# A two-layer hybrid decoder trunk: SiLU's table, the copies out of PSUM, the weight rounding and the small loads in another order

## What is computed

```python
for layer in range(DEPTH):
    h = rms_norm(x, norm_w[layer])
    proj = jnp.einsum('bsd,de->bse', h, w_in[layer])          # 4096 x 11792
    (g_q, g_k, g_v, g_a, s_q, s_k, s_v, d_q, d_k, d_v, r_x, gate) = split_cols(proj, IN_SPLITS)
    y = jnp.concatenate([gla_mixer(g_q, g_k, g_v, g_a, ...), swa_mixer(s_q, s_k, s_v, ...),
                         diff_mixer(d_q, d_k, d_v, ...), rglru_mixer(r_x, ...)], axis=-1)
    y = y * jax.nn.silu(gate)
    x = x + jnp.einsum('bse,ed->bsd', y, w_out[layer])        # 4096 x 4096
```

## Time and profile before

| | |
|---|---|
| median of 3 runs | 2942.19 us (2942.0 to 2942.79) |
| the profiled execution | 2942.81 us, span 2941.1 us |
| granted TensorE clock | 1.0 |
| TensorE matmul busy | 2913.7 us (99%) |
| VectorE busy | 1585.7 us (54%) |
| ScalarE busy | 1465.4 us (50%) |
| DMA | 546 MB, 186 GB/s over the span |

### The profile page before, as it was taken

The page is one execution under the profiler, slowest core; times in us unless marked ns, Lnnn a source line. Parts: engine busy times, 40 slices in busy tenths (PEclk is TensorE's granted clock), DMA queues, the critical chain, the costliest instruction groups (busy, mean ns, idle before and its releaser), DMA issues.

```text
span 2941.1 us, 34608 instructions
## 1 busy us (share of the span) xinstructions
PE 2913.7 (99%) x13381; PEld 2404.3 (82%) x13381; DVE 1585.7 (54%) x2098; ACT 1465.4 (50%) x2077; POOL 59.3 (2%) x106
## 2 busy tenths in 40 slices
PE   8999999999999999999999999999999999999999
PEld 6888888888888888888878888888888888888887
DVE  6545455555666446444554455555556664554444
ACT  5344455545556555444554444455555665553333
POOL 2000000000000000000000000000000000000000
PEclk9999999999999999999999999999999999999999
DMA  7665556666555665766666655566655555666665
GB/s 232 179 191 165 160 171 179 188 189 182 169 164 164 187 184 186 225 218 198 222 178 193 187 159 164 174 188 182 183 178 176 158 172 179 192 201 208 222 222 164
DMA packets 282964, 546.47 MB, mean 186 GB/s; under 512 B 17752, under 2 KB 22496, under 8 KB 282800
## 3 DMA queue, kind: packets, MB, share of 16 engines
q1 hardware_dynamic: 272560, 524.88, 58.1%
q0 software_dynamic: 5552, 17.26, 1.9%
q10 hardware_dynamic: 4688, 2.13, 0.3%
HBM read 535.81 MB, written 8.39 MB: 185 GB/s over the span
## 4 chain that ended last, share of the span: by engine, by line
PE 97%; ACT 1%; DMA 0%; DVE 0%; issue 0%; SPq 0%; ACTq 0%
PE main L1128 91%; PE mixer L1128 5%; ACT L382 1%; PE mixer L1343 0%; DMA w_raw<-in_w_in 0%; ACT stage L382 0%; DVE w_lo L697 0%; PE mixer L1168 0%; ACT w_hi L375 0%; PE mixer L1279 0%; PE mixer L1319 0%; PE mixer L1199 0%; PE mixer L1307 0%; PE mixer L1306 0%; PE mixer L1269 0%
## 5 line engine op out<-in xcount | busy, mean ns | idle before, releaser
L1128 PE MATMUL main<-w_hi,act 128*128 128x512 f32 x7936 | 2523.4, 394 | 17.1 <-ACT stage L382 13.6
L697 DVE TENSOR_TENSOR w_lo<-w_raw,w_hi 128x1024 fp32r<-128x1024 f32 x992 | 1204.8, 1224 | 1088.4 <-ACT w_hi L375 1081.5
L1128 PEld LDWEIGHTS main<-w_hi,act 128*128 128x128 f32 x7936 | 1491.0, 188 | 333.4 <-issue 19.9
L375 ACT ACTIVATE w_hi<-w_raw 128x1024 fp32r<-128x1024 f32 x992 | 1041.0, 1058 | 1070.2 <-PE main L1128 1039.5
L1128 PE MATMUL main<-w_lo,act 128*128 128x512 f32 x3968 | 1545.8, 390 | 0.0
L1128 PEld LDWEIGHTS main<-w_lo,act 128*128 128x128 f32 x3968 | 746.3, 188 | 149.2
L677 DVE SCALAR_TENSOR_TENSOR act<-act_T,par,act 128x256 fp32r<-128x256 f32 x96 | 42.0, 478 | 13.2 <-ACT act L357 13.1
L929 DVE TENSOR_TENSOR mix<-mix,main 128x512 f32<-128x512 f32 x32 | 22.0, 687 | 42.7 <-PE main L1128 42.7
L791 DVE TENSOR_SCALAR mix<-mix_Y,small 128x128 f32<-128x128 f32 x32 | 7.7, 282 | 67.7 <-ACT small L389 67.7
L357 ACT ACTIVATE act<-act_T,par 128x256 fp32r<-128x256 f32 x96 | 42.9, 495 | 0.1
L1128 PE MATMUL mixer<-act_T,mix 128*128 128x128 f32 (+1 forms) x256 | 39.6, 288 | 0.0
(11 more groups left out here) (238 smaller groups left out, 1092.4 us busy)
## 6 DMA issues: line engine op xcount, KB each, us to landing
w_raw<-in_w_in SPq DMA_DIRECT2D x736, 512.0 KB, 3.7
w_raw<-in_w_out SPq DMA_DIRECT2D x256, 512.0 KB, 3.7
out<-mix POOLq DMA_DIRECT2D x15, 512.0 KB, 3.2
mix<-in_x POOLq DMA_DIRECT2D x8, 512.0 KB, 6.0
mix<-out POOLq DMA_DIRECT2D x8, 512.0 KB, 5.9
mix_Y<-in_x SPq DMA_DIRECT2D x7, 512.0 KB, 9.2
act_T<-in_lru_w_r ACTq DMA_DIRECT2D x16, 64.0 KB, 2.6
act_T<-in_lru_w_i ACTq DMA_DIRECT2D x16, 64.0 KB, 2.7
```

Source lines behind the costliest of these rows:

```text
L375: act.activation(w_hi[:, n % HI, :, :], w_raw[:, n % RAW, :, :], ACT.Copy).then_inc(w_hi_ready, 1)
L697: dve.tensor_tensor(w_lo[:, n % LO, :, :], w_raw[:, n % RAW, :, :], w_hi[:, n % HI, :, :].bitcast(F32), ALU.subtract).then_inc(w_lo_ready, 1)
L1128: return pe.matmul(out_, lhsT, rhs, start=start, stop=stop, skip_group_check=True)
```

## The change

Five moves; no instruction of the computation is added or left out.

1. `preload_act_table_set("silu_and_others")` stands ahead of the waits of copy 0 of a gate chunk.
2. `project` and `evacuate` take the token half t: copy 0 is made at g = 0, copy 1 at g = 1. ScalarE's order becomes `hi(j,0)`, copy 0, what is hooked in at g = 0, `hi(j,1)`, copy 1, what is hooked in at g = 1.
3. In chunk 0 of layer 0 `hi` and `lo` run one group ahead: group 0's before the first split of x, group g + 1's at g, ahead of the split of x for g + 1.
4. The 23 row DMAs, and with them the first `load_rank`, wait for `w_used` 6 (six groups of chunk 0 done).
5. The rank product moves from the end of chunk 0 to the end of chunk 2 (`J_RANK` 2), its rounding to chunk 1 (g = 12 and 14) and the copy of its result to chunk 3.

Cut to its core:

```diff
+    J_RANK = J_GV
@@ gpsimd
-            def rows(dst, src):
-                pool.dma_start(dst, src).then_inc(rows_in, 16)
...
+            pool.wait_ge(w_used, 6)
+            def rows(dst, src):
+                pool.dma_start(dst, src).then_inc(rows_in, 16)
...
             load_rank(0)
@@ scalar
-            def evacuate(layer, j, dst, func):
+            def evacuate(layer, j, t, dst, func):
                 n = layer * CHUNKS + j
-                act.wait_ge(main0_ready, n + 1)
-                act.activation(dst[:, 0, :], main[0][:, :], func, scale=rstd[:, 0:1]).then_inc(main_free, 1)
-                act.wait_ge(w_used, n * NG + NG)
-                act.activation(dst[:, 1, :], main[1][:, :], func, scale=rstd[:, 1:2]).then_inc(main_free, 1)
+                if t == 0:
+                    act.wait_ge(main0_ready, n + 1)
+                else:
+                    act.wait_ge(w_used, n * NG + NG)
+                act.activation(dst[:, t, :], main[t][:, :], func, scale=rstd[:, t:t + 1]).then_inc(main_free, 1)
...
-            def project(layer, j, g):
-                if g != 1 or not 1 <= j <= J_OUT:
-                    return
+            def project(layer, j, t):
...
                 if done == J_GQ:
-                    evacuate(layer, done, gq, ACT.Copy)
+                    if t == 0:
+                        act.wait_ge(rs_ready, layer + 1)
+                    evacuate(layer, done, t, gq, ACT.Copy)
...
                 else:
-                    if done > J_GATE:
-                        act.wait_ge(gate_T, layer * 16 + (done - J_GATE) * 2)
-                    else:
-                        act.wait_ge(rx_T, layer * 4 + 4)
-                    evacuate(layer, done, stage, ACT.Silu)
-                    act.preload_act_table_set("natural_log_exp_and_others")
+                    if t == 0:
+                        act.preload_act_table_set("silu_and_others")
+                        if done > J_GATE:
+                            act.wait_ge(gate_T, layer * 16 + (done - J_GATE) * 2)
+                        else:
+                            act.wait_ge(rx_T, layer * 4 + 4)
+                    evacuate(layer, done, t, stage, ACT.Silu)
+                    if t:
+                        act.preload_act_table_set("natural_log_exp_and_others")
...
+            hi(0, 0, 0)
             act.wait_ge(norm_ready, 1)
             split_input_hi(0)
...
-                        hi(layer, j, g)
-                        project(layer, j, g)
+                        if layer or j:
+                            hi(layer, j, g)
+                        elif g < NG - 1:
+                            hi(0, 0, g + 1)
+                        if 1 <= j <= J_OUT and g < T:
+                            project(layer, j, g)
...
+                        if j == J_RANK - 1 and g == 12:
+                            act.wait_ge(wa_landed, layer * 16 + 16)
+                            act.activation(wa[:, :, 0:RANK], wa_raw, ACT.Copy).then_inc(wa_hi_ready, 1)
-                        if j == 1 and g == 3:
+                        if j == J_RANK + 1 and g == 3:
                             act.wait_ge(a_sum, layer + 1)
@@ vector
+            lo(0, 0, 0)
...
-                        lo(layer, j, g)
+                        if layer or j:
+                            lo(layer, j, g)
+                        elif g < NG - 1:
+                            lo(0, 0, g + 1)
...
+                        if j == J_RANK - 1 and g == 14:
+                            rank_lo(layer)
@@ tensor
-                        if j == 0 and g == NG - 1:
+                        if j == J_RANK and g == NG - 1:
                             rank(layer)
```

More of the change, by code:

```diff
@@ L332, in store_x @@
                                ).then_inc(x_stored, 16)
+            pool.wait_ge(w_used, 6)
+            def rows(dst, src):
+                pool.dma_start(dst, src).then_inc(rows_in, 16)
+            r1, r2 = MIX[:, 0:128], MIX[0:76, 128:256]
+            rows(r1[64:128, :], lru_conv_w.rearrange("l w (n p) -> (l w n) p", p=P))
+            for q, src in enumerate((lru_conv_b, lru_b_r, lru_b_i, lru_lambda)):
+                rows(r2[16 * q:16 * q + 16, :], src.rearrange("l (n p) -> (l n) p", p=P))
+            for q, src in enumerate((gla_norm_w, swa_q_norm, swa_k_norm, diff_out_norm)):
+                rows(r2[64 + 2 * q:66 + 2 * q, :], src)
+            for q, src in enumerate((diff_q_norm, diff_k_norm)):
+                for c in range(2):
+                    rows(r2[72 + 2 * q:74 + 2 * q, c * DK:(c + 1) * DK], src)
+            for l in range(DEPTH):
+                rows(par[:, l, Q_SINK:Q_SINK + HEADS], swa_sinks[l, :].partition_broadcast(P))
+                for q, src in enumerate((diff_lq1, diff_lk1, diff_lq2, diff_lk2)):
+                    rows(cut(512 + (4 * l + q) * DK, DK), src[l, :].partition_broadcast(P))
             load_rank(0)
@@ L579, in project @@
                 elif done == J_GK:
-                    evacuate(layer, done, gk, ACT.Copy)
+                    evacuate(layer, done, t, gk, ACT.Copy)
                 elif done < J_GV + 2:
                     base = (done - J_GV) * NC
-                    evacuate(layer, done, Y[:, :, base:base + NC], ACT.Copy)
+                    evacuate(layer, done, t, Y[:, :, base:base + NC], ACT.Copy)
                 elif done in J_SQ:
                     base = J_SQ.index(done) * NC + BW
-                    evacuate(layer, done, Y[:, :, base:base + NC], ACT.Copy)
+                    evacuate(layer, done, t, Y[:, :, base:base + NC], ACT.Copy)
@@ L587, in project @@
                 elif done in J_RX:
                     i = J_RX.index(done)
-                    if i:
+                    if t == 0 and i:
                         act.wait_ge(rx_T, layer * 4 + 2)
-                    elif layer:
+                    elif t == 0 and layer:
                         act.wait_ge(gate_T, layer * 16)
-                    evacuate(layer, done, stage, ACT.Copy)
-                    act.wait_ge(main_free, (layer * CHUNKS + done) * T + T)
-                    act.sem_inc(rx_out, 1)
+                    evacuate(layer, done, t, stage, ACT.Copy)
@@ L596, in project @@
+                    if t:
+                        act.wait_ge(main_free, evacuated(layer, done))
+                        act.sem_inc(rx_out, 1)
                 elif done == J_KV:
-                    evacuate(layer, done, skv, ACT.Copy)
+                    evacuate(layer, done, t, skv, ACT.Copy)
                 elif done < J_DK:
                     base = (done - J_DQ) * NC + 2 * BW
-                    evacuate(layer, done, Y[:, :, base:base + NC], ACT.Copy)
+                    evacuate(layer, done, t, Y[:, :, base:base + NC], ACT.Copy)
@@ L601, in project @@
                 elif done < J_DV:
                     base = (done - J_DK) * NC
-                    evacuate(layer, done, dk[:, :, base:base + NC], ACT.Copy)
+                    evacuate(layer, done, t, dk[:, :, base:base + NC], ACT.Copy)
                 elif done < J_GATE:
                     base = (done - J_DV) * NC
-                    evacuate(layer, done, dv[:, :, base:base + NC], ACT.Copy)
+                    evacuate(layer, done, t, dv[:, :, base:base + NC], ACT.Copy)
                 else:
-                    if done > J_GATE:
-                        act.wait_ge(gate_T, layer * 16 + (done - J_GATE) * 2)
-                    else:
-                        act.wait_ge(rx_T, layer * 4 + 4)
@@ L1080, in _ @@
                             parameters(g)
-                        if j == 1 and g == 4:
+                        if j == J_RANK - 1 and g == 14:
+                            rank_lo(layer)
+                        if j == J_RANK + 1 and g == 4:
                             dve.wait_ge(a_copied, layer + 1)
```

24 lines of the change are left out of this document (1 added, 23 removed).

## The result

The changed kernel takes 2925.83 us (median of 5 runs, 2925.4 to 2927.67) against 2942.19 (2941.73 to 2942.79): a ratio of 0.9945, 95% interval 0.9934 to 0.9956. The profiled execution took 2925.76 us, its span is 2924.0 against 2941.1, 17.1 less; the forecast was 2927, between 2920 and 2934.

What follows compares the result with a forecast made beforehand. Matmuls on TensorE were taken to set the time, so only waits before them could be won. Against the profiled 2942.8: -17.4 + 2.3 + 5.5 - 4.9 - 0.4 = -14.9, so 2927.9; median 0.6 lower, 2927.3, written 2927; range 2920 to 2934.

Steps and rivals of the forecast that it cites:

- The gates: At 16 gate boundaries, Silu's table load moves into idle time before E; 1.09 us won each at half 0, 17.4 us.
- E: Moment token half 0 of a chunk is done; at the first gate boundary Silu's table load began then, at 783.33.
- The yardstick: At every boundary, half 0's copy must end by E + 0.90, half 1's by E + 2.26; each us past is lost.
- Ordinary boundaries: At chunk boundaries without extra work between copies, half 1's copy ends at E + 2.23, inside 2.26 by 0.03: no loss.
- no overlap: Rival, chance 0.08: back-to-back ScalarE work doesn't overlap, half 1's copy ends at 2.44; 8.1 us more, 2935.4.
- LRU's term: At 16 LRU chunks, two DMA issues behind half 0's copy make half 1's 0.29 late; 5.5 us lost, one long issue included.
- The 0.87 for one long issue: One of 16 DMA issues at LRU chunks took 1.33 us, 0.87 more; counted as lost again in the new order.
- Issues pass the copy: Rival, chance 0.13: at LRU chunks DMA issues go out before E, past the waiting copy; the 5.5 falls away, 2921.8.
- The first output chunk: One a layer: `act` splits make copy 1 0.78 late, third group another 0.35; 1.13 lost each, 2.3 us in all.
- Long switch: Rival, chance 0.02: a table load holds ScalarE a second 1.28; half 1's copy 1.18 late at 8 boundaries, 9.4 more, 2936.7.
- Table displaced: Rival, chance 0.03: `w_hi` between the copies calls its own table back; 2.53 late at 16 gates, 2965.5, slower.
- Chunk 0: In chunk 0, weights rounded ahead of x's split end six `w_lo` waits: 4.9 us won, and some 0.4 of smaller ones.

## Why the prediction was right

The time was 1.2 below the forecast, and the mechanisms named are the ones that the runs show. Between the profiled executions the sum was 2.2 too small (17.1 for 14.9): 1.5 by LRU, 0.8 by chunk 0, less the 0.2 at chunk 28. The medians are 16.4 apart, and 0.3 of the forecast is the rounding of 2927.3 down, so that only 1.2 is left between forecast and median is in part luck.

*The gates.* E, the price of 1.09 per boundary and the number of 16 came out to the hundredth, and the run with the table behind the wait brought them back. That the load fits behind a diff head held with 0.08 to spare.

*The yardstick* (half 0's copy by E + 0.90, half 1's by E + 2.26) decided every other place. Ordinary boundaries were said to have 0.03 to spare and lose nothing: 0.00 to 0.03. The rival "no overlap" falls with it. (Its price for an LRU chunk, 0.21, is too high by its own terms: 1.06 for 0.95 gives 0.11 there, and 2933.8 for 2935.4.) LRU's term was mis-sized. Its step "the copy ends at 2.55" came out (454.49, E + 2.56); "0.29 late" did not. The second product stood at 454.88, 0.39 behind the copy's end and not 0.45, and it was due at E + 2.75 and not 2.71, as the run with the issues later shows (456.50, with E at 453.75). 2.56 + 0.39 - 2.75 is 0.20; measured are 0.21 at this product and 0.23 by the end of the group. In the diff chunks the prediction took the chunk before as 1.00 late at the scores, where it was 1.09; that would ask for `qkT` 0.09 sooner, and nothing was lost even so.

The 0.87 for one long issue did not come either; here are all 16 in the changed kernel (min/median/max ns):

```profile
L457 ACTq DMA_DIRECT2D act_T<-in_lru_w_i x16: 449/450/455, 404.6 to 2188.0; - x16
```

The 1326 ns in rows 6 belongs to a place and was no single event: the same issue, the first of the 16, took 1002 ns in the second execution of the kernel before and 862 with the split undone, and one in layer 1 took 659 and 767 in two of the runs with the issues moved. In all of these the issues stand behind `w_hi` (one more such trace, with the products ahead, has no long one); in the six traces in which they stand behind copy 0 none is over 0.46. Why is open. Carrying the 0.87 over into the new order was the mistake, of 0.9 us. Moving the issues showed that they are the whole of the loss.

*Issues pass the copy.* Refuted: the first issue starts at 451.93 with the copy, not before the moment it waits for. The sentence of the Trainium skill (Perfetto Trace Analysis, DVE / Act Engine Instruction), by which the sequencer would be free while the copy waits, doesn't describe these rows: what stands behind the waiting copy waited as well, and started within 0.03 of it at all 16 places.

*The first output chunk.* 0.78 and 0.35 were predicted, 0.72 and 0.37 measured, and both went when the splits moved.

*Long switch.* No drain is seen: the copy, which waits for E too, starts 0.08 behind a load of 1.28 that began 0.02 behind the rounding. The 2.66 us of the Trainium skill (ScalarE: Activation LUTs, What ACT_TABLE_LOAD costs) are not seen here. *Table displaced* falls too: `w_hi` at 779.80 stands between two copies under Silu's table with no load on either side, and there are 65 loads in either kernel.

*Chunk 0.* The order was given 5.3 and is worth 4.8 in groups 1 to 15. These are 5.6 shorter in all, so some 0.8 more came with what was taken as 0: the late rows, behind which weights landed sooner (the fourth group at 15.5 and 15.1 against 18.6 and 17.5), or the moved rank; the runs don't part the two in the old order. The first product did stand earlier in both pairs of executions (0.5 and 0.35), but at the start of group 1 the changed kernel was 0.5 ahead in one pair and 0.45 behind in the other, by the length of the slow stretch: taken as 0, this term was right on the mean of the two. One sign named as "wrong" did come: `w_hi` waits for landings (at 15.50 us, for 0.82). It cost nothing in the changed kernel, whose groups 1 to 13 take 3.20 or 3.21 each, but it did in the run with the rows at the start. "The rank product costs the same two chunks later" held but for two things: back in chunk 0 it costs 0.5 now that its weights come late, and moved it goes with the 0.2 at chunk 28.

## What to carry over

Where an engine stands idle before a wait and works behind it, ask for its table ahead of the wait: that gave 17.4 us here, chunk 0 some 6, and the split with what stood between the copies cost 6. A split or a reordering has to be priced at each kind of boundary, since work that stood harmlessly somewhere (two DMA issues, a pair of splits) lands between two copies that TensorE needs, and moving it on by two groups was free here. Compare the starts of the products, not the sums of waits, and take the first microseconds of a program apart, as chunk 1 started 0.5 us apart in two executions of one kernel, and up to 2.1 us apart in kernels whose chunk 0 is the same.

## What was not expected of the hardware

At the start products of 512 columns stood 0.43 us apart for 5 to 11 of them and then 0.23, while the view of the granted clock printed 1.00. The clock records of the trace settle it: the upper level begins at 11.09 to 15.73 us in the eleven traces without extra products, and at 7.45 with twelve of them ahead (24 instructions in the trace, as each takes two). Chunk 1 then started 2.0 us earlier than in the run compared, one of those with the longest slow stretch. 0.5 of that was lost again in pieces of 0.01 to 0.07, most of them in chunks 16 to 22, for a reason not found. Between the two executions of one kernel nothing behind the first chunk differed by more than 0.2 us in 2,860.
